# Gated linear attention in two chunks of 128 tokens instead of four of 64

## What is computed

```python
CHUNK = 64
def gla(q, k, v, log_a):
    ...
    bcum = jnp.cumsum(la, axis=2)
    b_last = bcum[:, :, -1]
    q_dec = qf * jnp.exp(bcum)
    k_inv = kf * jnp.exp(-bcum)
    k_end = kf * jnp.exp(b_last[:, :, None] - bcum)
    mask = jnp.tril(jnp.ones((CHUNK, CHUNK), dtype=bool))
    att = jnp.einsum('bnthk,bnshk->bnhts', q_dec, k_inv)
    att = jnp.where(mask, att, 0.0)
    o_intra = jnp.einsum('bnhts,bnshv->bnthv', att, vf)

    def step(state, xs):
        qd, ke, vc, bl = xs
        o = jnp.einsum('bthk,bhkv->bthv', qd, state)
        state = jnp.exp(bl)[..., None] * state + jnp.einsum('bshk,bshv->bhkv', ke, vc)
        return state, o
```

## Time and profile before

| | |
|---|---|
| median of 3 runs | 1046.85 us (1044.94 to 1047.94) |
| the profiled execution | 1045.93 us |
| its span, first to last instruction | 1044.2 us |
| busy: TensorE, VectorE, ScalarE, GpSimd | 1004.2, 723.6, 507.6, 41.7 us |
| granted TensorE clock, mean | 0.995 |
| read from HBM | 217.25 MB, 209 GB/s over the span |

### The profile page before, as it was taken

How to read it: one execution, slowest core, us unless ns; L and a number is a source line. 1 busy time by engine, 2 the same in 40 slices (tenths; PEclk the granted TensorE clock), 3 DMA queues, 4 the chain that set the end, 5 groups by cost and what they waited for, 6 DMA issues and landing times.

```text
span 1044.2 us, 19611 instructions
## 1 busy us (share of the span) xinstructions
PE 1004.2 (96%) x8234; PEld 991.3 (95%) x8234; DVE 723.6 (69%) x1027; ACT 507.6 (49%) x740; POOL 41.7 (4%) x69
## 2 busy tenths in 40 slices
PE   5999999999999999999999999999997999999998
PEld 5899999999999999999999999998997989999998
DVE  4867966777673856567889778667887665465554
ACT  2554354456524445634744464455556454444442
POOL 2100000000000003311000000000000000000000
PEclk9999999999999999999999999999999999999999
DMA  9987576657762884469467766755533446566621
GB/s 356 365 273 242 180 264 242 231 173 240 244 225 99 268 296 157 171 247 311 136 234 273 268 242 231 251 188 179 163 117 96 151 138 215 173 219 203 207 99 41
DMA packets 138960, 219.58 MB, mean 210 GB/s; under 512 B 7161, under 2 KB 110922, under 8 KB 138872
## 3 DMA queue, kind: packets, MB, share of 16 engines
q1 hardware_dynamic: 136776, 214.00, 59.5%
q10 hardware_dynamic: 1136, 2.58, 0.7%
q0 software_dynamic: 960, 1.76, 0.6%
HBM read 217.25 MB, written 1.05 MB: 209 GB/s over the span
## 4 chain that ended last, share of the span: by engine, by line
PE 84%; DVE 8%; ACT 3%; issue 2%; DMA 2%; SPq 1%; ACTq 0%; DVEq 0%
PE pw L550 62%; PE pacc L550 22%; DVE WL L1523 2%; DVE hl L1624 1%; DVE SQT L1619 1%; ACT AR L1083 1%; DMA ring<-in_even_in_w 1%; DVE ACC L1539 1%; DMA ring<-in_ada_w 1%; ACT hh L1083 0%; ACT WH L1083 0%; PE pw L930 0%; SPq L311 0%; DVE RS L1586 0%; ACT YH L1083 0%
## 5 line engine op out<-in xcount | busy, mean ns | idle before, releaser
L1083 ACT ACTIVATE WH<-ring 128x1024 fp32r<-128x1024 f32 x288 | 302.0, 1055 | 274.5 <-PE pw L550 194.5
L550 PE MATMUL pw<-hh,WH 128*128 128x256 f32 x1408 | 404.1, 287 | 8.8 <-DVE WL L1523 4.3
L1523 DVE TENSOR_TENSOR WL<-ring,WH 128x1024 fp32r<-128x1024 f32 x288 | 344.4, 1223 | 84.3 <-ACT WH L1083 83.8
L550 PE MATMUL pw<-hh,WL 128*128 128x256 f32 x1408 | 398.9, 283 | 0.0
L550 PE MATMUL pw<-hl,WH 128*128 128x256 f32 x1408 | 398.9, 283 | 0.0
L550 PEld LDWEIGHTS pw<-hh,WH 128*128 128x128 f32 x1408 | 270.6, 192 | 13.3 <-issue 10.2
L550 PEld LDWEIGHTS pw<-hl,WH 128*128 128x128 f32 x1408 | 270.7, 192 | 0.0
L550 PEld LDWEIGHTS pw<-hh,WL 128*128 128x128 f32 x1408 | 270.5, 192 | 0.0
L550 PE MATMUL pacc<-YH,WH 128*128 128x256 f32 x672 | 192.4, 286 | 3.5 <-issue 2.5
L550 PE MATMUL pacc<-YL,WH 128*128 128x256 f32 x672 | 190.8, 284 | 0.0
L550 PE MATMUL pacc<-YH,WL 128*128 128x256 f32 x672 | 190.8, 284 | 0.0
(11 more groups left out here) (245 smaller groups left out, 855.9 us busy)
## 6 DMA issues: line engine op xcount, KB each, us to landing
ring<-in_w_mod SPq DMA_DIRECT2D x72, 512.0 KB, 6.0
ring<-in_odd_in_w SPq DMA_DIRECT2D x56, 512.0 KB, 6.8
ring<-in_ada_w SPq DMA_DIRECT2D x48, 512.0 KB, 7.9
ring<-in_ffn_w_gate SPq DMA_DIRECT2D x44, 512.0 KB, 4.9
ring<-in_ffn_w_up SPq DMA_DIRECT2D x44, 512.0 KB, 5.2
ring<-in_ffn_w_down SPq DMA_DIRECT2D x44, 512.0 KB, 4.8
ring<-in_even_in_w SPq DMA_DIRECT2D x40, 512.0 KB, 6.9
ring<-in_even_out_w SPq DMA_DIRECT2D x16, 512.0 KB, 5.4
```

Source lines behind the costliest of these rows:

```text
L550: return eng.matmul(o, a, b, start=start, stop=stop, skip_group_check=True)
L1083: return eng.activation(dst, src, func, **kw)
L1523: tt(WL[:, i % NL, :], slot(half_of(i)), WH[:, i % NH, :].bitcast(F32), SUB).then_inc(s_lo, 1)
```

## The change

A chunk is now 128 tokens in two halves of 64, and the decay is still reckoned by halves. Inside a block of 128 tokens, keys of the first half against queries of the second half get a product of their own, `T3` (keys decayed to the half's end) with `GQ`, which overwrites that quarter of the attention block; the quarter is kept, and GpSimd's two memsets go. Only one state is left, that after the first 128 tokens. For it, `KE` holds the keys decayed to the block's end (first half: `T3` times the second half's whole decay; second half: `T3` as it is), and `QS` the queries of the second block decayed from the block's start. VectorE makes one half of each and ScalarE copies the other. `KE` is transposed (four transposes) behind `og0`, the state product stands behind `og1`, and `yc` behind `og2`, with six products of 128 columns per head.

```diff
+        KE, QS = (x.rearrange("p (h n) -> p h n", h=4)[:, :, 0:P] for x in (T1, T0))
+        EBH = EBL.rearrange("p (h c) -> p h c", c=4)
...
             for blk in range(2):
-                pb = open_(f"kt{blk}")
-                for h in range(4):
-                    last = eng.transpose(pb[:, h * P:h * P + P], T3[:, h * T + blk * P:h * T + blk * P + P], ident)
-                close(last, f"kt{blk}")
-            for blk in range(2):
                 pb = open_(f"at{blk}")
                 for h in range(4):
-                    sl = slice(h * T + blk * P, h * T + blk * P + P)
-                    last = mm(pb[:, h * P:h * P + P], T2[:, sl], GQ[:, sl])
+                    t0 = h * T + blk * P
+                    mm(pb[:, h * P:h * P + P], T2[:, t0:t0 + P], GQ[:, t0:t0 + P])
+                    last = mm(pb[0:64, h * P + 64:h * P + P], T3[:, t0:t0 + 64], GQ[:, t0 + 64:t0 + P])
                 close(last, f"at{blk}")
             gates = iter(range(8))
-            p.wait_ge(*gone["kt1"])
-            p.wait_ge(*gone["kt0"])
+            cols_T(L_ODD, f"og{next(gates)}")
+            p.wait_ge(s_kea, 1)
+            p.wait_ge(s_ked, 1)
+            pb = open_("kt")
+            for h in range(4):
+                last = eng.transpose(pb[:, h * P:h * P + P], KE[:, h, :], ident)
+            close(last, "kt")
+            cols_T(L_ODD, f"og{next(gates)}")
+            p.wait_ge(*gone["kt"])
             p.wait_ge(*gone["gv3"])
-            for c in range(3):
-                cols_T(L_ODD, f"og{next(gates)}")
-                rr = slice(64 * (c % 2), 64 * (c % 2) + 64)
-                for q in range(2):
-                    pb = open_(f"st{c}{q}", (s_st, 4 * c + 2 * q + 2))
-                    for m in range(2):
-                        h = 2 * q + m
-                        last = mm(pb[:, m * T:m * T + T], KT[rr, c // 2, h, :], GV[rr, c // 2, h * T:h * T + T])
-                    close(last, f"st{c}{q}")
+            for q in range(2):
+                pb = open_(f"st{q}", (s_st, 2 * q + 2))
+                for m in range(2):
+                    h = 2 * q + m
+                    last = mm(pb[:, m * T:m * T + T], KT[:, h, :], GV[:, 0, h * T:h * T + T])
+                close(last, f"st{q}")
             cols_T(L_ODD, f"og{next(gates)}")
...
             for h in range(4):
                 pb = open_(f"yc{h}")
                 for v in range(2):
+                    vs = slice(h * T + v * P, h * T + v * P + P)
                     for blk in range(2):
...
-                for v in range(2):
-                    for c in range(1, 4):
-                        p.wait_ge(s_st, 4 * c)
-                        last = mm(pb[:, v * T + 64 * c:v * T + 64 * c + 64], ST[c - 1][:, h, v * P:v * P + P],
-                                  GQ[:, h * T + 64 * c:h * T + 64 * c + 64], False, c == 3)
+                        mm(pb[:, v * T + blk * P:v * T + blk * P + P], GV[:, blk, vs], AT[:, blk, h, :],
+                           v == 0 and blk == 0, blk == 0)
+                    last = mm(pb[:, v * T + P:v * T + T], ST[:, h, v * P:v * P + P], QS[:, h, :], False, True)
                 close(last, f"yc{h}")
+            cols_T(L_ODD, f"og{next(gates)}")
             cols_T(L_ODD, f"og{next(gates)}")
```

On ScalarE, and on VectorE:

```diff
+            act(KE[:, :, 64:P], T3.rearrange("p (h n) -> p h n", h=4)[:, :, 64:P]).then_inc(s_kea, 1)
+            act(QS[:, :, 0:64], GQ.rearrange("p (h n) -> p h n", h=4)[:, :, P:P + 64]).then_inc(s_kea, 1)
...
-            for j in range(4):
-                gate(j)
+            gate(0)
+            evac("kt", KT, src=v3(pw[place["kt"]][:, :], 4))
+            gate(1)
+            gate(2)
...
-            for j in range(4, 8):
+            for j in range(3, 8):
                 gate(j)
...
+            tt(KE[:, :, 0:64], T3.rearrange("p (h n) -> p h n", h=4)[:, :, 0:64],
+               EBH[:, :, 1:2].to_broadcast([P, 4, 64]), MUL).then_inc(s_ked, 1)
+            tt(QS[:, :, 64:P], GQ.rearrange("p (h n) -> p h n", h=4)[:, :, P + 64:T],
+               EBH[:, :, 2:3].to_broadcast([P, 4, 64]), MUL).then_inc(s_ked, 1)
```

More of the change, by code:

```diff
@@ L384, in build @@
         s_st = sem("s_st")
+        s_kea, s_ked = sem("s_kea"), sem("s_ked")
         s_sc = sem("s_sc")
@@ L434, in build @@
         AT = T5.rearrange("p (b h t) -> p b h t", b=2, h=4)
-        KT = T4.rearrange("p (b h t) -> p b h t", b=2, h=4)
-        ST = [v3(GK, 4), v3(T0, 4), v3(T1, 4)]
+        KT = v3(T4[:, 0:512], 4)
+        ST = v3(GK, 4)
+        KE, QS = (x.rearrange("p (h n) -> p h n", h=4)[:, :, 0:P] for x in (T1, T0))
+        EBH = EBL.rearrange("p (h c) -> p h c", c=4)
         YC = v3(ar(16384, 2048), 8)
@@ L811, in _ @@
             for blk in range(2):
-                pb = open_(f"kt{blk}")
-                for h in range(4):
-                    last = eng.transpose(pb[:, h * P:h * P + P], T3[:, h * T + blk * P:h * T + blk * P + P], ident)
-                close(last, f"kt{blk}")
-            for blk in range(2):
                 pb = open_(f"at{blk}")
                 for h in range(4):
-                    sl = slice(h * T + blk * P, h * T + blk * P + P)
-                    last = mm(pb[:, h * P:h * P + P], T2[:, sl], GQ[:, sl])
+                    t0 = h * T + blk * P
+                    mm(pb[:, h * P:h * P + P], T2[:, t0:t0 + P], GQ[:, t0:t0 + P])
+                    last = mm(pb[0:64, h * P + 64:h * P + P], T3[:, t0:t0 + 64], GQ[:, t0 + 64:t0 + P])
                 close(last, f"at{blk}")
             gates = iter(range(8))
-            p.wait_ge(*gone["kt1"])
-            p.wait_ge(*gone["kt0"])
-            p.wait_ge(*gone["gv3"])
-            for c in range(3):
-                cols_T(L_ODD, f"og{next(gates)}")
-                rr = slice(64 * (c % 2), 64 * (c % 2) + 64)
-                for q in range(2):
-                    pb = open_(f"st{c}{q}", (s_st, 4 * c + 2 * q + 2))
-                    for m in range(2):
-                        h = 2 * q + m
-                        last = mm(pb[:, m * T:m * T + T], KT[rr, c // 2, h, :], GV[rr, c // 2, h * T:h * T + T])
-                    close(last, f"st{c}{q}")
+            cols_T(L_ODD, f"og{next(gates)}")
[7 more added lines that the diff above has]
+            p.wait_ge(*gone["kt"])
+            p.wait_ge(*gone["gv3"])
+            for q in range(2):
[4 more added lines that the diff above has]
+                close(last, f"st{q}")
             cols_T(L_ODD, f"og{next(gates)}")
             p.wait_ge(s_atm, 2)
+            p.wait_ge(s_kea, 2)
+            p.wait_ge(s_ked, 2)
+            p.wait_ge(s_st, 4)
             for h in range(4):
@@ L839, in _ @@
                 for v in range(2):
+                    vs = slice(h * T + v * P, h * T + v * P + P)
                     for blk in range(2):
-                        mm(pb[:, v * T + blk * P:v * T + blk * P + P], GV[:, blk, h * T + v * P:h * T + v * P + P],
-                           AT[:, blk, h, :], v == 0 and blk == 0, False)
-                for v in range(2):
-                    for c in range(1, 4):
-                        p.wait_ge(s_st, 4 * c)
-                        last = mm(pb[:, v * T + 64 * c:v * T + 64 * c + 64], ST[c - 1][:, h, v * P:v * P + P],
-                                  GQ[:, h * T + 64 * c:h * T + 64 * c + 64], False, c == 3)
+                        mm(pb[:, v * T + blk * P:v * T + blk * P + P], GV[:, blk, vs], AT[:, blk, h, :],
+                           v == 0 and blk == 0, blk == 0)
+                    last = mm(pb[:, v * T + P:v * T + T], ST[:, h, v * P:v * P + P], QS[:, h, :], False, True)
                 close(last, f"yc{h}")
+            cols_T(L_ODD, f"og{next(gates)}")
             cols_T(L_ODD, f"og{next(gates)}")
@@ L1245, in _ @@
             eng.preload_act_table_set("silu_and_others")
-            s.wait_ge(s_dla, 2)
-            for blk in range(2):
-                evac(f"kt{blk}", KT[:, blk], src=v3(pw[place[f"kt{blk}"]][:, :], 4))
+            s.wait_ge(s_kqe, 3)
+            act(KE[:, :, 64:P], T3.rearrange("p (h n) -> p h n", h=4)[:, :, 64:P]).then_inc(s_kea, 1)
+            act(QS[:, :, 0:64], GQ.rearrange("p (h n) -> p h n", h=4)[:, :, P:P + 64]).then_inc(s_kea, 1)
             s.wait_ge(s_bc, 1)
@@ L1808, in _ @@
             v.wait_ge(s_ebl, 1)
[L1809 to L1821, removed]
+            tt(KE[:, :, 0:64], T3.rearrange("p (h n) -> p h n", h=4)[:, :, 0:64],
+               EBH[:, :, 1:2].to_broadcast([P, 4, 64]), MUL).then_inc(s_ked, 1)
+            tt(QS[:, :, 64:P], GQ.rearrange("p (h n) -> p h n", h=4)[:, :, P + 64:T],
+               EBH[:, :, 2:3].to_broadcast([P, 4, 64]), MUL).then_inc(s_ked, 1)
+            pieces(f"og{next(gates)}")
+            pieces(f"og{next(gates)}")
+            for q in range(2):
+                pb = pw[place[f"st{q}"]]
+                v.wait_ge(*full[f"st{q}"])
+                for m in range(2):
+                    eng.tensor_copy(ST[:, 2 * q + m, :], pb[:, m * T:m * T + T]).then_inc(s_st, 1)
+            pieces(f"og{next(gates)}")
```

(3 more changed lines are left out.)

## The result

The changed kernel took 1042.37 us in the median of six runs (1039.42 to 1043.35), the one before 1046.91 in six (1044.94 to 1048.44). The ratio is 0.9946 with an interval of 0.9930 to 0.9962, half a per cent faster; the two medians are 4.5 us apart. The profiled execution took 1039.80 us with a span of 1038.1, against 1045.93 and 1044.2 before: 6.1 less.

What follows compares the result with a forecast made beforehand. TensorE, busy 96% of the span, was taken as the bound. `at` +1.15, `kt` +0.44, `st` -4.2, `yc` -3.5 and one entry less -0.1 gave -6.2 us: 1046.85 to 1040.6 us, range 1038.3 to 1043.0.

Steps and rivals of the forecast that it cites:

- `at`, forecast 4.4 us: Attention block products: eight full ones each get a 64-column partner, alternating; 4.4 us against 3.25 before, so +1.15.
- 0.11 to the second record: First item of an `at` pair: the full product's second record starts 0.11 us after its first.
- The two edges: In each `at` pair, the steps out of the full product, 0.20 us, and out of the partner, 0.15 us.
- The partner's record s: Time of one record of the 64-column product in `at`: taken as 0.08 us, bounded by 0.055 and 0.111.
- `st`, forecast 1.8: State products: three steps and their edges in, 6.03 us, become one 128-row step of 1.8 us; -4.2.
- `yc`, -3.5: `yc` goes from 40 products to 24; sixteen times 0.221 us saved, -3.5 us.
- Transposes: Key transposes on TensorE: eight become four, behind `og0`, taking 0.44 us instead of 0.88.
- the wait of 0.43: TensorE's 0.43 us wait for ScalarE's evacuation of the transposed keys, expected to go.
- `og3` and `og4` together: With these two units adjacent, one entry less from f32 products to projections: -0.1 us.
- What must stay hidden: Work on other engines costs nothing; nearest to a wait is `gate(3)` moved later on ScalarE, 3 us to spare before `og4`.
- The second rival: ScalarE or VectorE late behind `yc`, 3 to 6 us of the gain lost: 1043.8 to 1046.8 us; 7%.
- The first rival (no edges): Alternation in `at` costs nothing: 2.7 to 3.6 us there, -7.0 to -7.9 in all, about 1039.5 us; 25%.

Runs made afterwards that it cites:

- full width: Changed kernel, but each 64-column partner product in `at` loads all 128 columns of `T3` as weights: 1039.84 us, ratio 0.9929 to the kernel before.
- grouping: Changed kernel, but in each `at` block the four full products come first, then the four 64-column partners: 1039.82 us, ratio 0.9927 to the kernel before.
- `yc` split: Changed kernel, but the state's part of `yc` is two products of 64 columns instead of one of 128: 1042.60 us, ratio 0.9954 to the kernel before.

## Why the prediction was right, point by point

The forecast was 1040.6 us in 1038.3 to 1043.0 and -6.2 in the profiled execution; measured were 1042.4, which is 4.5 below the median before (5.65 by the ratio), and -6.1.

- *What bounds the kernel.* Right. 5.66 of the 6.1 us are in the stretch, and no wait of TensorE behind it grew. That 6.1 stands beside 6.2 is in part luck: 0.37 of it came before the change, and in the stretch, forecast 43.0 and measured 43.50, `at` came out 0.9 dearer, which the cheaper `st` and `yc` made good in part.
- *`at`, forecast 4.4 us, the term that was mis-sized.* The mechanism was right, and full width and grouping show it: the changes of form cost, not the overwriting. The size was 0.9 short, 5.31. The item of a pair that was mis-sized is the first, "0.11 to the second record". Behind an edge it is 0.21, 0.1 more in seven pairs. The two edges were right, 0.20 and 0.15. The partner's record s was 0.11 rather than 0.08, since in a pair its first record pays too; only in a group is it 0.06. The pair came out at 0.68, above the bounds of 0.51 to 0.64 (the lower of which is 0.47 by the values named for it, 0.11+0.15+0.055+0.15). The 0.1 was in the rows: the prediction took the record of 0.48 in the earlier trace rows for the last of the `st` step, and it is the first, behind the edge (the row at 286.05, above). So that step pays 0.1 on its first record, and its way out is 0.30, not 0.41. The price of 0.216 a record came out right only because the two slips cancel.
- *`st`, forecast 1.8.* 1.54, and 0.1 of it shows up behind. The records come every 0.216, as forecast; what was too high is the end: the first record of `og2` starts 0.03 after the last one of the step (297.15 to 297.18) and the next 0.31 later, where the forecast had a whole record and 0.08.
- *`yc`, -3.5.* -3.57, and `yc` split shows why: with 128 weight columns it is products that count, 0.22 us each here, not whether they move 64 or 128 columns.
- *Transposes, the wait of 0.43, `og3` and `og4` together.* As forecast: 0.44, no wait, 11.59 us for the two units (308.40 to 319.99).
- *What must stay hidden.* 3 us to spare were forecast, 3.2 measured, and the wait beyond them is 4.73 for 4.6. The second rival's price was too low, though: in this one execution a loss of 4.7 us by waiting came with 2.4 more at a granted clock of 0.50.
- *The first rival (no edges)* wanted 2.7 to 3.6 us for `at`. It gets there only where the changes go: 3.29 with four of them (grouped) and 3.49 with none (full width). `gl`'s rows, which spoke for it, are f32r products; f32 ones behave otherwise here (0.11 in for `gl`, 0.21 in for f32 with 32 weight columns), and no run separates the dtype from the 16 columns. What goes on inside TensorE at a change of form, whether its pipeline restarts as the prediction says, no run shows. What the runs show is that weight load and matmul start together there (276.81, 277.06), and what a change costs, 0.17 us by the grouped kernel. The partner's 0.058 a record in the group is near the prediction's lower bound for s, 0.055.
- *The median against the trace.* The 6.2 us were taken from one execution and laid on a median, with 1 us allowed for the scatter. The scatter is larger. The changed kernel's twelve runs are 1039.24 to 1039.80 us at a mean clock of 0.995 or 0.996 (four), 1041.64 and 1041.67 at 0.993, and 1042.77 to 1043.35 at 0.991 (six). So the median of each six lies between the second and the third group, the first one 2.6 us above its profiled execution and 1.8 above the forecast. Four of the twelve runs are above 1043.0: that the median is inside the range hangs also on how the runs fell into the groups.

## What to carry to other kernels

An f32 product with 128 weight columns took 0.22 us with 64 and with 128 moving columns alike, so halving them buys nothing: count products, and merge narrow ones. An f32 product that uses 64 of the array's columns should not alternate with full ones (0.17 us a change here); group them, or load the full width where what it adds does no harm, or rearrange the scaling so that it isn't needed. And a step that is moved behind others on a helper engine is free only up to its spare time: reckon that from the trace, and remember that a wait beyond it may not be the whole loss: behind the 4.73 us here the granted clock was 0.50, and 2.4 us more were gone.

## What the runs showed of the hardware

The granted clock does not fall at the same places in each execution. Two executions of the changed kernel in the windows view, by stretches of ten us; first that with a span of 1038.1 us:

```profile
35.00:45.00 10.00, 7.90 (x53) 7.93 (x54) 8.82 (x22) 7.38 (x12) 0.00 (x0) 0.83 1.07 360
140.00:150.00 10.00, 8.20 (x67) 7.83 (x66) 7.18 (x8) 6.21 (x11) 0.00 (x0) 1.00 0.87 295
640.00:650.00 10.00, 10.00 (x84) 10.00 (x85) 9.89 (x9) 3.18 (x3) 0.00 (x0) 1.00 0.89 314
785.00:795.00 10.00, 6.72 (x44) 6.53 (x44) 7.77 (x20) 3.90 (x8) 0.00 (x0) 0.83 0.50 153
```

Then that with a span of 1041.5:

```profile
35.00:45.00 10.00, 7.68 (x59) 7.40 (x60) 8.81 (x22) 7.38 (x12) 0.00 (x0) 1.00 1.06 357
140.00:150.00 10.00, 8.55 (x59) 8.58 (x60) 6.58 (x7) 5.49 (x10) 0.00 (x0) 0.83 0.93 314
640.00:650.00 10.00, 9.34 (x65) 9.37 (x66) 9.90 (x9) 2.12 (x2) 0.00 (x0) 0.83 0.89 298
785.00:795.00 10.00, 6.72 (x43) 6.36 (x42) 8.66 (x18) 5.30 (x11) 0.00 (x0) 0.80 0.49 137
```

In each of these stretches, or just ahead of it, TensorE waits. In the first execution the waits are 2.22 us before 37.10 (for `hl`), 1.77 before 142.15, 2.10 before 639.88, and 1.93 and 1.36 before the squares' sums at 786.95 and 789.44. The second has the same ones, of the same length within 0.06 us. Behind the first wait the clock is at 0.50 for a time (39 to 41 us) in the first execution and stays at 1.00 in the second. Behind the next two it is the other way round: 0.50 from 143 to 145 and from 641 to 644 us in the second, 1.00 in the first. Around the last ones it falls in both, to 0.50 from 790 to 792 us in the first and from 791 to 797 in the second. What decides that was not tried.
